# Three edits to an eight-core decoder trunk: norm log and exp as a pair, one weight sum on VectorE, last gates and output projection tile by tile

## The chip, the cores and the metric

The kernel runs on the eight cores of one Trainium2 chip, one launch, no exchange between the cores: each takes one of the eight prompt sequences (2048 tokens) and 16 of the 128 sample sequences (8 tokens each, 128 columns). A core has TensorE (PE: matmuls, PEld its weight loads), VectorE (DVE), ScalarE (ACT), GpSimd (POOL) and SyncE (SP). The metric is the device time in microseconds of the slowest core.

## The reference

```python
def layer(x, c, ...):
    mod = jax.nn.silu(c) @ w_ada + b_ada                 # nine vectors of 1024 for each sequence
    h = rmsnorm(x, n1) * (1 + sc1) + sh1
    x = x + 0.5 * gt1 * swiglu(h, f1g, f1u, f1d)         # 1024 -> 2816 -> 1024
    h = rmsnorm(x, nm) * (1 + sc2) + sh2
    y, ... = token_mixer(h, ...)
    x = x + gt2 * y
    h = rmsnorm(x, n2) * (1 + sc3) + sh3
    x = x + 0.5 * gt3 * swiglu(h, f2g, f2u, f2d)

def token_mixer(h, ...):
    xp, xl, gl, u, v, gates = split(h @ w_in)
    y_pool = pool_mixer(xp, ...); y_lru = rg_lru(causal_conv(xl), ...) * gelu(gl); y_gm = chunk_gmlp(u, v, ...)
    g = sigmoid(gates)                                   # three gates of 1024 channels
    merged = g[0] * (y_pool @ wbo_pool) + g[1] * (y_lru @ wbo_lru) + g[2] * (y_gm @ wbo_gm)
    return merged @ w_out
```

There are four layers and one last RMSNorm. rmsnorm(x) = x * rsqrt(mean(x*x) + 1e-6) * g. New states of pool, convolution and recurrence are outputs too.

## The kernel before

**Tiling.** Activations lie with channels on the partitions: `xT` (f32, the residual stream), `hT` (bf16, the normed input), and three bf16 buffers, seen in the order listings as `R0` (the merged mixer output), `R1`, `R2` (during the last gates the recurrent branch's output); the profile writes all three as `R`. The columns are worked off in two groups. The first is two prompt tiles of 512 columns (called tile 0 and tile 1 here), the second is two more and the sample tile of 128. Each group goes through all four layers: first FFN, mixer, output projection, second FFN. So there are eight passes of each stage.

**A norm.** Each of the eight 128-channel chunks of `xT` is squared on ScalarE; the squares are added on GpSimd, except that the last goes to TensorE beside the sum (`sbt,onesb` matmuls, a mean over channels). Then `rstd` (L818) makes `exp(-0.5*ln(mean+eps))` by two ScalarE activations, which both have the table set lnexp; eight chunks are multiplied by it (two on GpSimd, six on VectorE), and scaled and shifted into `hT` (six on ScalarE, two on VectorE). In an FFN `tsums` (L906) then makes four sums and differences of parts of `hT` on VectorE (L903), since the gate and up products are made by a Strassen-Winograd scheme of seven products of half size.

**Weights** come over GpSimd's DMA queue, converted to bf16, into a ring of 84 pages of 256 columns (`wload`, L671). A gate/up block has 4096 columns and takes 7168, because `wino_load` (L687) adds four sums of 1024: two on VectorE, the third by `W3_ENG`, the fourth by `W4_ENG`, both GpSimd before. An FFN loads 11 such blocks. The first two are used for tile 0, then for the other tiles (`units`, L983 to L986), so that the last tile's norm has matmuls beside it.

**The mixer's end** (L1402 on). For gate branch 1, which reads the recurrent output, channels 0 to 3 are done for all tiles, then 4 to 7 for tile 0, then 4 to 7 for tile 1 (and the sample tile). One `gate_unit` of a prompt tile is eight matmuls on `hT`, eight on `R2`, a tanh on ScalarE, a product on VectorE and an addition into `R0` on GpSimd. Then comes the projection: for each tile eight times eight matmuls on `R0`, each followed by the residual sum into `xT` on VectorE and by the norm's square. Every group of eight needs all eight chunks of `R0` of its tile.

**What sets the order.** All operations are recorded in program order with their dependencies. `schedule` (L247) then runs a list scheduler with cost estimates, and each engine's instructions are written out in the order in which it picked them. Among the ready ones it takes the first by program order for which a PSUM bank or a scratch buffer is free. On ScalarE it passes over an activation whose table set is not loaded, as long as another can run, unless it has been ready for `PATIENCE` (L326). On the chip each engine runs its own list strictly in order, and waits on semaphores.

## Time and profile before

| | |
|---|---|
| three runs | 6855.04, 7126.43, 7339.58 us; median 7126.43 us |
| profiled execution | 6869.45 us, slowest core 7 with a span of 6867.9 us, others from 6830.3 us |
| TensorE | busy 6475.0 us (94%), 46336 matmuls |
| VectorE | busy 3873.2 us (56%) |
| ScalarE | busy 3234.2 us (47%) |
| GpSimd | busy 2576.4 us (38%) |
| granted TensorE clock, core 7 | 0.975 of full speed |
| weights by GpSimd's queue | 539.01 MB, 44.4% of 16 DMA engines |

The page gives for each engine the busy time of the slowest core; a busy TensorE includes matmuls that run at a lower clock. The chain of waits goes back from the last instruction to whatever released each one; 80% of it is matmuls, 7% VectorE, 4% ScalarE, 2% DMA and 6% issue. A timeline row is a run of equal instructions with its start and its duration, and in brackets the idle time of the engine ahead of it and what ended that.

### The profile page before, as it was taken

To read this page: it belongs to the slowest core of one execution; us is meant where nothing else is said; L and a number is where in the kernel's file an instruction comes from. 1 tells how busy PE (TensorE), PEld (TensorE's weight loads), DVE (VectorE), ACT (ScalarE), POOL (GpSimd) and SP (SyncE) were. 2 spreads that over 40 slices of the span, in tenths; PEclk is the share of its full clock that TensorE was granted. 3 is DMA by queue.
4 is the path that set the end of the run, shared out by engine and by line. 5 is a ranking of instruction groups with operands and counts; after the bars stand their busy time and mean duration, and the time that the engine had idled before them with its cause. 6 is when DMAs were issued, how large, how long until landed. Compare 5 with 4: busy or idle time off the path is not lost.

```text
span 6867.9 us, 135354 instructions; the slowest of 8 cores (6830.3 to 6867.9 us)
## 1 busy us (share of the span) xinstructions
PE 6475.0 (94%) x46336; PEld 4093.9 (60%) x46336; DVE 3873.2 (56%) x6064; ACT 3234.2 (47%) x6151; POOL 2576.4 (38%) x2626
## 2 busy tenths in 40 slices
PE   5999999999999999999999999999999999999999
PEld 4644765456744666447754586644767447674466
DVE  4364664655655654755647465464744756556564
ACT  3274444633455433744447444374533744336542
POOL 3245333443334433353433433334322344233442
PEclk9899999999999999999999999999999999999999
DMA  6775546645557356435544342434334443343423
GB/s 123 112 120 100 90 88 119 111 80 108 94 102 127 63 100 119 81 61 97 125 75 93 65 83 54 83 78 77 66 64 77 84 83 58 66 84 73 83 54 81
DMA packets 146674, 600.93 MB, mean 87 GB/s; under 512 B 20944, under 2 KB 53200, under 8 KB 104016
## 3 DMA queue, kind: packets, MB, share of 16 engines
q0 software_dynamic: 89856, 539.01, 44.4%
q1 hardware_dynamic: 56144, 53.27, 3.0%
q8 instruction: 383, 6.28, 0.4%
q14 instruction: 291, 2.38, 0.1%
HBM read 1109.23 MB, written 21.95 MB: 165 GB/s over the span
## 4 chain that ended last, share of the span: by engine, by line
PE 80%; DVE 7%; issue 6%; ACT 4%; DMA 2%; POOL 1%; SPq 1%; DVEq 0%; ACTq 0%; POOLq 0%
PE psum L559 80%; ACT sbt L581 3%; DVE sbt L590 2%; DVE sbt L605 1%; DMA ring<-ffn_gu 1%; DVE sbt L620 1%; ACT L581 1%; DVE xT L605 1%; SPq L627 1%; DVE hT L598 0%; DVE sbt L903 0%; DMA xT<-xp 0%; DVE hT L903 0%; DVE psum L590 0%; POOL sbt L611 0%
## 5 line engine op out<-in xcount | busy, mean ns | idle before, releaser
L559 PE MATMUL psum<-hT,ring 128*128 128x256 bf16 (+2 forms) x21696 | 3207.2, 301 | 175.9 <-ACT sbt L581 32.4
L559 PEld LDWEIGHTS psum<-hT,ring 128*128 128x128 bf16 x21696 | 1994.8, 99 | 1152.8 <-issue 241.0
L581 ACT ACTIVATE sbt<-psum 128x512 f32<-128x512 f32 (+2 forms) x3229 | 1566.0, 509 | 1791.1 <-PE psum L559 1317.1
L559 PE MATMUL psum<-R,ring 128*128 128x512 bf16 (+1 forms) x11520 | 2207.0, 348 | 1.0 <-ACT R L581 0.9
L559 PEld LDWEIGHTS psum<-R,ring 128*128 128x128 bf16 x11520 | 1032.0, 98 | 1083.8 <-issue 28.7
L559 PE MATMUL psum<-sbt,ring 128*128 128x256 bf16 (+2 forms) x9792 | 1307.0, 278 | 107.6 <-ACT sbt L581 50.5
L559 PEld LDWEIGHTS psum<-sbt,ring 128*128 128x128 bf16 x9792 | 934.7, 99 | 322.8 <-issue 158.9
L646 POOL TENSOR_TENSOR ring<-ring 128x1024 bf16<-128x1024 bf16 x352 | 756.6, 2167 | 585.2 <-DVE ring L646 580.2
L605 DVE SCALAR_TENSOR_TENSOR xT<-psum,modT,xT 128x512 f32<-128x512 f32 x384 | 284.0, 748 | 936.1 <-PE psum L559 936.1
L581 ACT ACTIVATE sbt<-xT 128x512 f32<-128x512 f32 (+1 forms) x426 | 266.3, 628 | 1071.6 <-DVE xT L605 992.2
L590 DVE TENSOR_TENSOR psum<-psum,sbt 128x512 f32<-128x512 f32 x704 | 489.8, 697 | 354.8 <-ACT sbt L581 244.6
L590 POOL TENSOR_TENSOR sbt<-sbt 128x512 f32<-128x512 f32 (+1 forms) x316 | 414.9, 1314 | 717.2 <-ACT sbt L581 695.3
L590 DVE TENSOR_TENSOR R<-sbt,psum 128x256 bf16<-128x256 f32 x1144 | 473.4, 416 | 243.8 <-ACT sbt L581 231.4
L605 DVE SCALAR_TENSOR_TENSOR sbt<-sbt,psum 128x512 f32<-128x512 f32 (+1 forms) x288 | 188.4, 656 | 538.9 <-PE psum L559 469.5
L590 POOL TENSOR_TENSOR R<-R,sbt 128x512 bf16<-128x512 bf16 (+1 forms) x288 | 339.1, 1179 | 382.2 <-DVE sbt L605 373.3
L605 DVE SCALAR_TENSOR_TENSOR sbt<-sbt,vecT 128x512 f32<-128x512 f32 (+1 forms) x480 | 348.1, 743 | 134.4 <-ACT convst L581 83.5
L605 DVE SCALAR_TENSOR_TENSOR sbt<-sbt 128x512 f32<-128x512 f32 (+2 forms) x448 | 316.3, 726 | 183.7 <-ACT sbt L581 176.2
L581 ACT ACTIVATE sbt<-sbt 128x256 f32<-128x256 f32 (+1 forms) x577 | 269.9, 482 | 270.5 <-DVE sbt L590 257.8
L581 ACT ACT_TABLE_LOAD x266 | 341.3, 1283 | 116.9 <-PE psum L559 92.5
L590 DVE TENSOR_TENSOR sbt<-xT,sbt 128x512 f32<-128x512 f32 x300 | 323.5, 1128 | 68.4 <-ACT sbt L581 67.7
L627 POOL DMA_DIRECT2D ring<-ffn_gu x176 | 99.7, 567 | 673.2 <-PE psum L559 646.4
L590 DVE TENSOR_TENSOR R<-sbt 128x256 bf16<-128x256 f32 x352 | 212.1, 603 | 152.3 <-ACT sbt L581 150.0
(84 smaller groups left out, 3824.4 us busy)
## 6 DMA issues: line engine op xcount, KB each, us to landing
ring<-ffn_gu POOLq DMA_DIRECT2D x176, 1024.0 KB, 8.9
ring<-ffn_dn POOLq DMA_DIRECT2D x128, 704.0 KB, 8.4
ring<-ada_w POOLq DMA_DIRECT2D x72, 1024.0 KB, 10.7
ring<-w_gate POOLq DMA_DIRECT2D x64, 1024.0 KB, 9.8
ring<-w_lru POOLq DMA_DIRECT2D x64, 576.0 KB, 8.8
ring<-w_gate POOLq DMA_DIRECT2D x32, 768.0 KB, 9.7
ring<-w_pool POOLq DMA_DIRECT2D x32, 640.0 KB, 8.5
ring<-w_o POOLq DMA_DIRECT2D x32, 512.0 KB, 9.6
```

Of the source, the lines that this page charges most:

```text
L559: ins = e.matmul(res(o), lhsT=res(l), rhs=res(r), start=st, stop=sp, skip_group_check=shared)
L581: return S.add("act", lambda e: e.activation(out=res(out), in_=res(in_), func=func, **{k: res(v) for k, v in kw.items()}), reads=rd, write ...
L590: return S.add(eng, lambda e: e.tensor_tensor(out=res(out), in0=res(in0), in1=res(in1), op=op), reads=[in0, in1], writes=[out], cost=dcost ...
L605: return S.add(eng, lambda e: e.scalar_tensor_tensor(out=res(out), in0=res(in0), scalar=scalar, in1=res(in1), op0=op0, op1=op1), reads=rd, ...
L620: return S.add("dve", lambda e: e.tensor_tensor_scan(out=res(out), data0=res(d0), data1=res(d1), initial=res(init), op0=op0, op1=op1), rea ...
L627: return S.add(q, lambda e: e.dma_start(out=res(out), in_=res(in_), **kw), reads=[in_] if reads is None else reads, writes=[out] if writes ...
L646: self.op.append(S.add(eng, lambda e: e.tensor_tensor(out=self.ap, in0=a, in1=b, op=op), reads=[a, b], writes=[self.ap], cost=160.0 + 0.6 ...
```

## The change

Three things are edited. **(1)** In `rstd` both activations are marked urgent: the scheduler may pick them even if their table set is not loaded, and it keeps ScalarE shut for another 25 ns of its own reckoning after the log, so that the exp, ready by then, is the next pick. `PATIENCE` of the others goes from 5000 to 10000. **(2)** The third weight sum of each gate/up block goes to VectorE. **(3)** Gate branch 1 is done for channels 0 to 5 of all tiles; channels 6 and 7 are done tile by tile, each tile's just ahead of its own projection. The load of the last gate block is now recorded behind those of the projection. In the FFN the two hooks, which may each record one step of the conditioning vectors (`ada_slot`), move ahead by one pass of the loop.

```diff
@@ -35,7 +35,7 @@
 HOLD = 4
 ADA0 = {"gu": 0.46, "dn": 1, "mix": 0.5}
 ADA1 = {"dn": 1, "mix": 0.39}
-W3_ENG = "pool"
+W3_ENG = "dve"
 W4_ENG = "pool"
 
 O_XP, O_XL, O_GL, O_U, O_V, O_G0 = 0, 1024, 2048, 3072, 3584, 4096
@@ -131,7 +131,7 @@
 
 class Op:
     __slots__ = ("eng", "fn", "dma", "deps", "signal", "count", "sem", "target", "prev", "cost", "tset",
-                 "prio", "nbytes", "alloc", "pvs", "succ", "nd", "start", "ready", "lat", "idx", "stage")
+                 "prio", "nbytes", "alloc", "pvs", "succ", "nd", "start", "ready", "lat", "idx", "stage", "urgent", "hold")
 
     def __init__(self, eng, fn, dma):
         self.eng, self.fn, self.dma = eng, fn, dma
@@ -141,6 +141,8 @@
         self.sem = None
         self.target = 0
         self.prev = 0
+        self.urgent = False
+        self.hold = 0.0
 
 
 class Sched:
@@ -150,7 +152,7 @@
     PE_LAT = 210.0
     SEM_LAT = 70.0
     TABLE = 1300.0
-    PATIENCE = 5000.0
+    PATIENCE = 10000.0
     RES = {"b": 1, "s": 4}
 
     def __init__(self):
@@ -323,7 +325,7 @@
                         if not can(o):
                             skipped.append(it)
                             continue
-                        if e == "act" and not (o.tset is None or table in o.tset
+                        if e == "act" and not (o.tset is None or table in o.tset or o.urgent
                                                or now - o.ready > self.PATIENCE):
                             if late is None:
                                 late = it
@@ -354,7 +356,7 @@
                         c += self.TABLE
                         table = o.tset[0]
                     o.start = now
-                    free_at[e] = now + c
+                    free_at[e] = now + c + o.hold
                     busy[e] += c
                     self.ops[e].append(o)
                     if o.dma:
@@ -364,7 +366,7 @@
                     else:
                         fin = now + c + (self.PE_LAT if e == "pe" else 0.0)
                     push(fin, 0, o)
-                    push(now + c, 2, o)
+                    push(now + c + o.hold, 2, o)
                 for it in waiting[e]:
                     if it[2].ready == 0.0:
                         it[2].ready = now
@@ -819,8 +821,9 @@
             assert self.k == KC
             r = SB()
             n = self.t.n
-            act(r.f(n), self.pv.c(n), AF.Ln, bias=EPS, scale=1.0)
-            act(r.f(n), r.f(n), AF.Exp, scale=-0.5)
+            ln = act(r.f(n), self.pv.c(n), AF.Ln, bias=EPS, scale=1.0)
+            ln.urgent, ln.hold = True, 25.0
+            act(r.f(n), r.f(n), AF.Exp, scale=-0.5).urgent = True
             return r
 
     def norm_apply(l, which, nm):
@@ -984,8 +987,7 @@
             units(first[jb], jb, grp[:1])
         for jb in range(2):
             units(first[jb], jb, grp[1:])
-        hook("gu")
-        hook("gu")
+            hook("gu")
         for jb in range(2, 11):
             units(wino_load(gu[l, jb], len(grp)), jb, grp)
             hook("gu")
@@ -1399,17 +1401,15 @@
         if last_prompt:
             dma(o_conv_p[l], convst[:, l])
             dma(o_lru_p[l], lrust[:, l])
-        for c, f in gates(1, KC, ylr, range(4)):
+        for c, f in gates(1, KC, ylr, range(6)):
             f()
-        for t in grp:
-            for c, f in gates(1, KC, ylr, range(4, 8), [t]):
-                f()
-
         S.stage = S.stage.replace('mix','wo')
         next_mod(l, 2)
         wos = [wload(w_o[l, q], 2048, 2 * len(grp)) for q in range(4)]
         hook()
         for t in grp:
+            for c, f in gates(1, KC, ylr, range(6, 8), [t]):
+                f()
             nm = Norm(t)
             for m in range(KC):
                 n = t.n
```

The order of the instructions moves with it. **The first place** is the projection of layer 1 in the first group. On TensorE `psum<-hT` x8 with `psum<-R2` x8 is one gate unit, `psum<-R0` the projection (64 for each tile), `sbt,onesb` the norm's mean, the 256-column rows the second FFN. Before:

```order
L559 MATMUL psum<-hT,ring 128x512 x8
L559 MATMUL psum<-R2,ring 128x512 x8
L559 MATMUL psum<-hT,ring 128x512 x8
L559 MATMUL psum<-R2,ring 128x512 x8
L559 MATMUL psum<-hT,ring 128x512 x8
L559 MATMUL psum<-R2,ring 128x512 x8
L559 MATMUL psum<-scT,ring 128x17 x32
L559 MATMUL psum<-R0,ring 128x512 x88
L559 MATMUL psum<-sbt,onesb 128x512 x2
L559 MATMUL psum<-R0,ring 128x512 x40
L559 MATMUL psum<-hT,ring 128x256 x32
L559 MATMUL psum<-sbt,ring 128x256 x16
```

And with the change (line numbers are two higher in the new file):

```order
L561 MATMUL psum<-hT,ring 128x512 x8
L561 MATMUL psum<-R2,ring 128x512 x8
L561 MATMUL psum<-hT,ring 128x512 x8
L561 MATMUL psum<-R2,ring 128x512 x8
L561 MATMUL psum<-R0,ring 128x512 x8
L561 MATMUL psum<-scT,ring 128x17 x32
L561 MATMUL psum<-R0,ring 128x512 x56
L561 MATMUL psum<-hT,ring 128x512 x8
L561 MATMUL psum<-R2,ring 128x512 x8
L561 MATMUL psum<-sbt,onesb 128x512 x2
L561 MATMUL psum<-R0,ring 128x512 x64
L561 MATMUL psum<-hT,ring 128x256 x40
```

The gate units of tile 1 stood all ahead of the first projection. Now one of them stands behind tile 0's 64 matmuls, and right behind it the projection of tile 1, whose input it makes, with only two norm matmuls between. On ScalarE the same place has the log (`sbt<-psum`, one) and the exp (`sbt<-sbt`) of tile 0's norm. Before:

```order
L581 ACTIVATE sbt<-psum 128x512 x22
L581 ACTIVATE sbt<-xT 128x512 x10
L581 ACTIVATE sbt<-psum 128x512
L581 ACTIVATE sbt<-xT 128x512
L581 ACTIVATE sbt<-sbt 128x512
L581 ACTIVATE sbt<-xT 128x512
L581 ACTIVATE hT<-sbt,modT 128x512 x6
```

With the change:

```order
L583 ACTIVATE sbt<-psum 128x512 x22
L583 ACTIVATE sbt<-xT 128x512 x8
L583 ACTIVATE sbt<-psum 128x512 x2
L583 ACTIVATE sbt<-sbt 128x512
L583 ACTIVATE hT<-sbt,modT 128x512 x6
```

A square of tile 1 stood between log and exp, and one more behind the exp ahead of the first scaled chunk (`hT<-sbt,modT`). Neither does now; the log is the second of the two `sbt<-psum`, behind a gate's tanh.

**The second place** is GpSimd's queue there: `R0<-R0,sbt` are the gates' additions, `sbt<-sbt` the norm's sums, `sbt<-xT,sbt` its products, `ring<-ring` weight sums, DMA rows weight loads. Before:

```order
L590 TENSOR_TENSOR R0<-R0,sbt 128x512 x5
L627 DMA ring<-ffn2_gu 128x4096
L590 TENSOR_TENSOR R0<-R0,sbt 128x512 x3
L627 DMA ring<-ffn2_gu 128x4096
L590 TENSOR_TENSOR sbt<-sbt 128x512 x3
L646 TENSOR_TENSOR ring<-ring 128x1024
L590 TENSOR_TENSOR sbt<-sbt 128x512
L646 TENSOR_TENSOR ring<-ring 128x1024
L590 TENSOR_TENSOR sbt<-sbt 128x512 x4
L590 TENSOR_TENSOR sbt<-xT,sbt 128x512 x2
```

With the change:

```order
L592 TENSOR_TENSOR R0<-R0,sbt 128x512 x4
L629 DMA ring<-ffn2_gu 128x4096
L592 TENSOR_TENSOR sbt<-sbt 128x512 x6
L629 DMA ring<-ffn2_gu 128x4096
L592 TENSOR_TENSOR R0<-R0,sbt 128x512
L592 TENSOR_TENSOR sbt<-xT,sbt 128x512 x2
L592 TENSOR_TENSOR sbt<-sbt 128x512 x2
L629 DMA ring<-ffn2_gu 128x4096
L592 TENSOR_TENSOR sbt<-sbt 128x512
L648 TENSOR_TENSOR ring<-ring 128x1024
```

Both loads of the coming FFN stood ahead of the norm's sums of tile 0. Now the second stands behind six of them, and the third ahead of the last sums of tile 1; tile 0's sums are no longer parted by weight sums.

**The third place** is ScalarE at the change from the second FFN to the next layer's first, in the second group (layers 0 and 1). `128x128` rows are the sample tile's log (`sbt<-psum`) and exp (`sbt<-sbt`); 128x256 rows are the FFN's silu or, where read from PSUM, also copies for its products. Before:

```order
L581 ACTIVATE sbt<-psum 128x256
L581 ACTIVATE sbt<-xT 128x512
L581 ACTIVATE sbt<-psum 128x512 x2
L581 ACTIVATE sbt<-psum 128x128
L581 ACTIVATE sbt<-psum 128x256 x2
L581 ACTIVATE sbt<-sbt 128x256
L581 ACTIVATE sbt<-psum 128x512 x2
L581 ACTIVATE sbt<-sbt 128x128
L581 ACTIVATE sbt<-psum 128x512 x2
L581 ACTIVATE sbt<-psum 128x256 x3
```

With the change:

```order
L583 ACTIVATE sbt<-psum 128x256
L583 ACTIVATE sbt<-xT 128x512
L583 ACTIVATE sbt<-psum 128x512
L583 ACTIVATE sbt<-psum 128x128
L583 ACTIVATE sbt<-sbt 128x128
L583 ACTIVATE sbt<-psum 128x512
L583 ACTIVATE sbt<-psum 128x256
L583 ACTIVATE sbt<-psum 128x512 x2
L583 ACTIVATE sbt<-psum 128x256 x2
```

Between log and exp stood five activations of the FFN, among them two runs of 256-column ones; now they follow each other.

## Rows read from the trace of the kernel before

**Rows 1.** Windows over the span, core 7; the first row names the columns.

```profile
core 7: us, PE busy (x) PEld busy (x) DVE busy (x) ACT busy (x) POOL busy (x), PEclk, DMA share, GB/s
...
200.00:6800.00 6600.00, 6307.97 (x44946) 3973.64 (x44944) 3760.71 (x5860) 3148.27 (x5983) 2500.57 (x2543) 0.98 0.47 87
```

**Rows 2.** Window inside the second FFN of layer 1, first group.

```profile
1600.00:1720.00 120.00, 119.35 (x847) 73.17 (x844) 50.30 (x85) 35.83 (x70) 40.03 (x36) 1.00 0.65 113
```

**Rows 3.** Windows at the eight changes from projection to second FFN.

```profile
1478.00:1528.00 50.00, 37.22 (x263) 27.44 (x262) 41.90 (x58) 28.84 (x51) 18.38 (x14) 0.86 0.20 34
...
4822.00:4852.00 30.00, 17.77 (x142) 13.13 (x140) 27.56 (x35) 19.24 (x32) 14.48 (x9) 0.83 0.22 41
...
sum 324.00, PE 222.65 PEld 164.53 DVE 281.32 ACT 190.57 POOL 132.60; mean PE 27.83 PEld 20.57 DVE 35.16 ACT 23.82 POOL 16.58
```

**Rows 4.** Timeline of TensorE at the projection of layer 1, first group.

```profile
1453.02 19.15 PE L559 MATMUL psum<-R,ring 128*128 128x512 bf16 x88
...
1482.46 1.03 PE L559 MATMUL psum<-hT,ring 128*128 128x256 bf16 x8 [1.11 <-ACT hT L581]
1486.42 3.54 PE L559 MATMUL psum<-hT,ring 128*128 128x256 bf16 x16 [2.93 <-DVE xT L605]
...
1505.58 1.03 PE L559 MATMUL psum<-hT,ring 128*128 128x256 bf16 x8 [2.90 <-ACT hT L581]
1508.69 1.87 PE L559 MATMUL psum<-hT,ring 128*128 128x256 bf16 x8 [2.08 <-DVE psum L590]
```

**Rows 5.** Timeline of VectorE, same place: norm products, then residual sums.

```profile
1476.01 4.63 DVE L590 TENSOR_TENSOR sbt<-xT,sbt 128x512 f32<-128x512 f32 x3 [0.70 <-ACT sbt L581]
...
1481.96 1.88 DVE L590 TENSOR_TENSOR sbt<-xT,sbt 128x512 f32<-128x512 f32 x3
...
1484.23 2.71 DVE L605 SCALAR_TENSOR_TENSOR xT<-psum,modT,xT 128x512 f32<-128x512 f32 x4
```

**Rows 6.** Timeline of ScalarE, same place: table load; square between log and exp.

```profile
1472.91 1.28 ACT L581 ACT_TABLE_LOAD   x1 [0.77 <-PE psum L559]
...
1474.69 0.62 ACT L581 ACTIVATE sbt<-xT 128x512 f32<-128x512 f32 x1
```

**Rows 7.** Timeline of GpSimd, same place: weight sum, tile 0's last norm sum.

```profile
1466.47 2.13 POOL L646 TENSOR_TENSOR ring<-ring 128x1024 bf16<-128x1024 bf16 x1
...
1470.49 1.27 POOL L590 TENSOR_TENSOR sbt<-sbt 128x512 bf16<-128x512 f32 x1 [0.20 <-POOL sbt L590]
```

**Rows 8.** Timeline: a gate unit's last matmuls and its addition.

```profile
644.30 1.89 PE L559 MATMUL psum<-R,ring 128*128 128x512 bf16 x8
...
647.20 1.16 POOL L590 TENSOR_TENSOR R<-R,sbt 128x512 bf16<-128x512 bf16 x1 [2.16 <-DVE sbt L605]
```

**Rows 9.** Timeline of ScalarE and TensorE, second group, second FFN to layer 1.

```profile
4200.19 1.28 ACT L581 ACT_TABLE_LOAD   x1
...
4212.90 1.28 ACT L581 ACT_TABLE_LOAD   x1 [0.20 <-PE psum L559]
...
4219.39 1.03 PE L559 MATMUL psum<-sbt,ring 128*128 128x256 bf16 x8 [4.06 <-ACT sbt L581]
```

**Rows 10.** Windows at changes from second FFN to the next layer.

```profile
926.00:941.00 15.00, 8.58 (x48) 5.56 (x47) 13.64 (x19) 7.37 (x13) 5.31 (x3) 0.63 0.01 2
...
4187.00:4222.00 35.00, 24.87 (x239) 20.60 (x237) 28.92 (x41) 21.44 (x34) 9.37 (x7) 0.93 0.30 52
```

**Rows 11.** Groups of instructions by line: weight sums and table loads.

```profile
L646 POOL TENSOR_TENSOR ring<-ring 128x1024 bf16<-128x1024 bf16 x352 | 756.6, 2167 | 585.2 <-DVE ring L646 580.2
...
L646 DVE TENSOR_TENSOR ring<-ring 128x1024 bf16<-128x1024 bf16 x352 | 254.7, 724 | 29.6 <-DMA ring<-ffn_gu 11.8 <-DVE ring L646 10.7 <-PE psum L559 4.0
...
L581 ACT ACT_TABLE_LOAD x266 | 341.3, 1283 | 116.9 <-PE psum L559 92.5
```

**Rows 12.** TensorE's waits for FFN weights, whole span: total, times, longest.

```profile
PE psum L559 <- DMA ring<-ffn_gu: 24.9, 6, 14.3
```

**Rows 13.** The page's part 6: count, KB each, median us to landing.

```profile
ring<-ffn_gu POOLq DMA_DIRECT2D x176, 1024.0 KB, 8.9
```


## The prediction

> **What bounds the kernel now.** I read the windows over the span first. Between 200 and 6800 us TensorE is busy 6307.97 us and idle 292 us, at a mean granted clock of 0.98 [rows 1]. So the whole prize is 292 us of idleness and about 2% of clock; no edit here removes matmuls. Then a window inside an FFN: TensorE 119.35 of 120 us at clock 1.00, VectorE 50.30, GpSimd 40.03 [rows 2]. There nothing but matmuls counts, and a sum moved between the other two engines is free. The idleness lies where the stages change. In the eight windows from the projection to the second FFN TensorE works 222.65 of 324 us, so 101.35 us are idle, 12.7 us at each change, and VectorE is busy 281.32 us, 87% [rows 3]. The clock falls there as well: 0.86 and 0.83 in the two windows shown, against 1.00 in the FFN [rows 2, 3]. That is 50 x 0.14 + 30 x 0.17 = 12.1 us of full-speed work beside 12.78 + 12.23 = 25.0 us of idleness, 0.48 us for each idle us. Since part of a dip belongs to gaps that stay, I let each idle us saved give back 0.4 us more; the factor is 1.4.
>
> Next the timelines at one such change, layer 1 of the first group. The last 88 projection matmuls start at 1453.02 and take 19.15 us, 0.218 us each; 40 more follow [rows 4]. The FFN starts with gaps of 1.11 us (for a scaled chunk of tile 0) and 2.93 us (for the sums behind it), and for tile 1 it waits 2.90 and 2.08 us more [rows 4]. VectorE shows why: tile 0's norm products come in two runs, and four residual sums of tile 1, whose matmuls were done, stand behind them and start at 1484.23 only [rows 5]. Tile 1's norm begins with those.
>
> **Edit 3, gates tile by tile.** The order puts one gate unit of tile 1, 16 matmuls or 16 x 0.218 = 3.48 us, between tile 0's projection and tile 1's. Tile 0's norm has that much more beside it. The change adds a wait, however: tile 1's projection needs the eighth merged chunk, which that unit makes. From the end of its matmuls (644.30 + 1.89 = 646.19) to the end of the addition on GpSimd (647.20 + 1.16 = 648.36) it takes 2.17 us [rows 8]; two norm matmuls cover 0.44, and TensorE, which has all the projection and the FFN queued behind, waits about 1.7 us. Tile 0's norm gains 3.48 + 1.7 = 5.2 us of cover against 1.11 + 2.93 = 4.04 us of gap, so the gap goes: 4.04 - 1.7 = 2.3 us gained. Tile 1's residual sums no longer queue behind the norm: their last ends with its matmuls, at about 1481.2 + 1.7 + 1.0 = 1483.9 instead of 1484.23 + 2.71 = 1486.94 [rows 4, 5], 3.0 us earlier, and nearly all that follows hangs on it. I take 2.5 us for each of the four changes in the first group. In the second group the sample tile's gate unit stands behind tile 1's, so the addition is covered and I take the full 3.5 us, again four times. Sum 24 us of idleness. The nearest bounds are 0 (norm still late) and 4.04 us at each.
>
> The gate's own product and addition are not new work, they move into a crowded stretch: one product on VectorE, one addition of 1.16 us on GpSimd. In return GpSimd's queue loses two weight sums of 2.13 us that stood among tile 0's norm sums, the last of which ended at 1471.76 [rows 7]. I set these against each other.
>
> **Edit 1, log and exp as a pair.** In the order a square stood between them; in the trace it starts at 1474.69, while the log's table load had begun 0.77 us after ScalarE went idle for the norm's matmuls [rows 6]. The square takes 0.62 us, of which about 0.5 us come through, since neighbours overlap a little. Only the last norm of a change hangs on the path: 8 changes into the second FFN, 8 into the mixer, 6 into the next layer, so 22 x 0.5 = 11 us. From a second FFN to the next layer TensorE is idle 15 - 8.58 = 6.4 us in the first group and 35 - 24.87 = 10.1 us in the second, where the sample tile's norm comes last [rows 10]. At the third place of the order, five FFN activations parted the sample tile's log and exp. There the trace has five table loads between 4200.19 and 4214.2, the first and the last of which are shown, and TensorE then waits 4.06 us for ScalarE [rows 9]. With the pair two of the five loads go, 2 x 1.283 us [rows 11]; three such changes at 2.5 us give 7.5 us. `PATIENCE` decides on ties of waiting activations alone; ScalarE has room between changes, so I cost it at nothing, and if that cover is gone at a change it is one load, 1.28 us.
>
> The Trainium skill speaks against this edit (page "ScalarE: Activation LUTs", section "Table sets: the hidden batching unit"): do all activations of one table set before changing to another; a log taken at once breaks into a run of silu. By that rule each norm pays a further pair of loads and the sum comes out near 6900 us instead of 6808; it is a rival below. The page's price of a load, about 1283 ns, the trace bears out [rows 11]; that a log held back saves one, it does not, since the log starts a load as soon as its input is there [rows 6].
>
> **Edit 2, third weight sum.** 176 sums of 2167 ns leave GpSimd, and 176 of 724 ns come to VectorE [rows 11], 127 us in all. Most stand inside an FFN, where VectorE has 70 of 120 us free [rows 2]: nothing. If that cover were gone, all 127 us would count. At the eight changes it is two-sided. VectorE gets two such sums in its crowded stretch (1.4 us); but three norm products take 4.63 us while GpSimd works on its own and 1.88 us when it does not [rows 5], so less work on GpSimd is worth up to 2.75 us. I take the middle, 1.0 us for each, 8 us.
>
> **What gets worse.** Weight loads. The load of the last gate block and the coming FFN's second block move back in GpSimd's queue; the second now stands behind six norm sums of tile 0, where both stood ahead of all of them. It has the rest of tile 0's projection and tile 1's 64 matmuls (14 us) before TensorE wants it, against 8.9 us to land [rows 13] and a few sums of 0.72 and 2.17 us: just enough. TensorE's waits for FFN weights are 24.9 us in six times, longest 14.3 [rows 12]. The trace has no such load at this place; between 0 and 5 us at each change, I take 1.25 us each, 10 us, nearer to nothing because it fits by count. The mixer's other reordering I take at nothing, within 10 us either way: its gaps are small pieces. The hooks shift work, they add none.
>
> **Sum.** Idleness 24 + 11 + 7.5 + 8 = 50.5 us, with the clock 1.4 x 50.5 = 71 us; less 10 us for late weights: 61 us. Against the profiled execution, 6869.45 us with its span of 6867.9, that is **6808 us**, 0.9% less. This execution is near the lowest of the three runs shown (6855.04); their median, 7126.43, lies 3.7% above it. The same ratio on that median would be 7063 us.
>
> **Rivals.**
> - *VectorE takes the place of the wait.* It is busy 87% of those windows, 27.56 of 30 us in one [rows 3]. Then cover on TensorE does not help, and two weight sums and a gate's product there cost 2 us each time: 8 x 2 x 1.4 = 22 us back, 24 x 1.4 = 34 us not gained, 11 not gained for edit 2. 6808 + 67 = 6875 us. Against it: its idle-free run holds norm products slowed by GpSimd. Chance 0.20.
> - *Weights come too late* (the slower side). Place: the start of each second FFN, where the second block is loaded behind tile 0's norm sums. The gains of 71 us are used up when each of eight loads comes 71 / (8 x 1.4) = 6.3 us late. With 10 us each, which the longest wait of 14.3 us [rows 12] allows, it is 112 us lost instead of 10: 6910 us. Against it: few waits for weights now. Chance 0.12.
> - *The batching rule holds.* 22 norms on the path with a pair of loads each, 2 x 1.283 us [rows 11]: 22 x 2.57 x 1.4 = 79 us, and the 15 us of log and exp are not gained: about 6900 us. Chance 0.05.
> - *Both tiles' gaps close.* Once the norms are not held up by each other, all 101.35 us at the eight changes go: 142 us with the clock, instead of 1.4 x 32 = 45. 6808 - 97 = 6711 us. Chance 0.08.
> - *The forecast*: 0.55, with 6770 to 6845 us as its own range.
>
> **Numbers.** The range goes from 6740, half way to all gaps closing, to 7070, which takes in the slower cases on the profiled execution and the forecast on the median of the runs shown. About 2% is what a measurement of this kernel can tell from no change. Below 6732 us lies only the rival with both gaps closed and a corner of the forecast: faster by over 2% 0.10. Over 7007 us needs late weights of 18 us at each change, or work that VectorE never catches up: 0.05. Within 2%: 0.85.
>
> **What would show it.** In the changed profile: (a) the same eight changes idle about 75 us instead of 101, with a clock near 0.88; (b) a gap of 1.5 to 2 us ahead of tile 1's projection in the first group, and none ahead of tile 0's first FFN matmuls; (c) tile 1's residual sums singly, each behind its matmuls, not four in a run; (d) exp right behind log, three table loads instead of five at the third place; (e) VectorE busy 100 to 127 us more in all, GpSimd 380 less, the FFN's inside still over 99% TensorE; (f) waits for FFN weights up by about 10 us. It is wrong if (b)'s second gap stays, if weights take (f) past 60 us, or if gaps open inside the mixer, which I have not costed.

## The result

The profiled execution of the changed kernel took 6779.97 us (slowest core 6, span 6778.4 us; the others from 6761.0 us), against 6869.45 us before. The ratio to the kernel before is **0.9892 [0.985, 0.9935]**, and in a second set of runs (e5 below) 0.9895 [0.9867, 0.9924]: 1.1% faster, between the 0.9% of the forecast (61 us) and the 1.3% between the two profiled executions (89 us). The median of all four runs, 7365.86 us, holds executions in which the cores of one die ran at a granted clock of 0.85 to 0.91; the ratio and the times named below leave them out.

### The profile page after: what moved, and what is told of

Same layout as the page of the kernel before. It is cut to its first block, busy times and chain, and to the rows that moved or that the text cites. A ratio compares the mean times of both kernels' runs of the same rounds, so it can differ in the third digit from the quotient of the medians.

```text
span 6778.4 us, 134693 instructions; the slowest of 8 cores (6761.0 to 6778.4 us)
## 1 busy us (share of the span) xinstructions
PE 6392.8 (94%) x45887; PEld 4069.7 (60%) x46336; DVE 4034.8 (60%) x6240; ACT 3228.0 (48%) x6143; POOL 2203.1 (33%) x2450
## 4 chain that ended last, share of the span: by engine, by line
PE 79%; issue 6%; DVE 6%; ACT 5%; DMA 1%; POOL 1%; SPq 1%; DVEq 0%; ACTq 0%; POOLq 0%
PE psum L561 79%; ACT sbt L583 3%; DVE sbt L592 2%; DVE sbt L607 1%; DVE psum L592 1%; ACT L583 1%; DVE xT L607 1%; DVE sbt L622 1%; DMA ring<-ffn_gu 1%; SPq L629 1%; DVE sbt L906 1%; DVE ring L648 0%; ACT hT L583 0%; DMA xT<-xp 0%; DVE hT L906 0%
## 5 line engine op out<-in xcount | busy, mean ns | idle before, releaser
L561 PE MATMUL psum<-hT,ring 128*128 128x256 bf16 (+2 forms) x21522 | 3148.3, 298 | 140.0 <-ACT sbt L583 29.8
L561 PEld LDWEIGHTS psum<-hT,ring 128*128 128x128 bf16 x21696 | 1974.1, 99 | 1090.4 <-issue 195.9
L561 PE MATMUL psum<-sbt,ring 128*128 128x256 bf16 (+2 forms) x9774 | 1285.9, 276 | 90.0 <-ACT sbt L583 34.1
L648 POOL TENSOR_TENSOR ring<-ring 128x1024 bf16<-128x1024 bf16 x176 | 392.1, 2228 | 584.0 <-DVE ring L648 497.8
L648 DVE TENSOR_TENSOR ring<-ring 128x1024 bf16<-128x1024 bf16 x528 | 491.5, 931 | 39.2 <-DMA ring<-ffn_gu 20.9
L583 ACT ACTIVATE sbt<-sbt 128x256 f32<-128x256 f32 (+2 forms) x577 | 270.5, 482 | 270.7 <-DVE sbt L592 251.4
L592 DVE TENSOR_TENSOR sbt<-xT,sbt 128x512 f32<-128x512 f32 x300 | 309.7, 1083 | 94.9 <-ACT sbt L583 94.9
```

The source lines that it names most:

```text
L561: ins = e.matmul(res(o), lhsT=res(l), rhs=res(r), start=st, stop=sp, skip_group_check=shared)
L583: return S.add("act", lambda e: e.activation(out=res(out), in_=res(in_), func=func, **{k: res(v) for k, v in kw.items()}), reads=rd, write ...
L592: return S.add(eng, lambda e: e.tensor_tensor(out=res(out), in0=res(in0), in1=res(in1), op=op), reads=[in0, in1], writes=[out], cost=dcost ...
L648: self.op.append(S.add(eng, lambda e: e.tensor_tensor(out=self.ap, in0=a, in1=b, op=op), reads=[a, b], writes=[self.ap], cost=160.0 + 0.6 ...
```

## The profile after

From the page of the changed kernel: busy time by engine, and the weight sums (three of a block's four on VectorE now, the fourth on GpSimd).

```profile
PE 6392.8 (94%) x45887; PEld 4069.7 (60%) x46336; DVE 4034.8 (60%) x6240; ACT 3228.0 (48%) x6143; POOL 2203.1 (33%) x2450
...
L648 POOL TENSOR_TENSOR ring<-ring 128x1024 bf16<-128x1024 bf16 x176 | 392.1, 2228 | 584.0 <-DVE ring L648 497.8
L648 DVE TENSOR_TENSOR ring<-ring 128x1024 bf16<-128x1024 bf16 x528 | 491.5, 931 | 39.2 <-DMA ring<-ffn_gu 20.9
```

GpSimd lost 373 us of work. VectorE got 162 us more, not 127: its sums take 931 ns on average where they took 724 [rows 11]. Now the eight windows from projection to second FFN, at the same distances from the FFN's first matmul as in [rows 3] (columns as there); layer 1 of each group is shown.

```profile
1433.00:1483.00 50.00, 40.14 (x303) 30.91 (x302) 44.46 (x63) 27.98 (x52) 20.74 (x14) 0.90 0.14 25
...
4756.00:4786.00 30.00, 25.86 (x238) 21.72 (x236) 28.14 (x46) 19.42 (x38) 5.19 (x4) 0.94 0.23 44
...
sum 324.00, PE 268.84 PEld 217.09 DVE 283.13 ACT 193.54 POOL 96.98; mean PE 33.60 PEld 27.14 DVE 35.39 ACT 24.19 POOL 12.12
```

TensorE is idle 324 - 268.84 = 55.2 us there, not 101.35. But part of that has moved ahead of the windows. TensorE's timeline at layer 1, first group (answers to [rows 4]), and then one row of the second group:

```profile
1420.65 0.59 PE L561 MATMUL psum<-sbt,onesb 128*128 128x512 bf16 x2
1423.36 13.97 PE L561 MATMUL psum<-R,ring 128*128 128x512 bf16 x63 [2.12 <-POOL R L592]
1437.17 2.96 PE L561 MATMUL psum<-hT,ring 128*128 128x256 bf16 x24
1445.56 3.39 PE L561 MATMUL psum<-hT,ring 128*128 128x256 bf16 x16 [5.43 <-ACT sbt L583]
...
4754.57 0.63 PE L561 MATMUL psum<-sbt,onesb 128*128 128x512 bf16 x1 [3.89 <-DVE sbt L906]
```

The wait for the eighth merged chunk is there (2.12 us), tile 0's first FFN matmuls start at once, and 24 matmuls later TensorE stops for 5.43 us. In the second group 3.89 us now lie ahead of the FFN. All four layers of each group have such a wait: 1.99 to 2.12 us in the first, 3.89 to 3.92 us in the second. VectorE (answers to [rows 5]) and GpSimd, same place:

```profile
1424.22 4.07 DVE L592 TENSOR_TENSOR sbt<-xT,sbt 128x512 f32<-128x512 f32 x3 [2.54 <-ACT sbt L583]
...
1428.66 1.88 DVE L592 TENSOR_TENSOR sbt<-xT,sbt 128x512 f32<-128x512 f32 x3
...
1430.92 3.37 DVE L607 SCALAR_TENSOR_TENSOR xT<-psum,modT,xT 128x512 f32<-128x512 f32 x5
...
1437.28 4.55 DVE L648 TENSOR_TENSOR ring<-ring 128x1024 bf16<-128x1024 bf16 x1
1441.75 1.74 DVE L906 TENSOR_TENSOR sbt<-hT 128x1024 bf16<-128x1024 bf16 x1
1443.42 0.74 DVE L607 SCALAR_TENSOR_TENSOR xT<-psum,modT,xT 128x512 f32<-128x512 f32 x1
```

```profile
1436.70 1.28 POOL L592 TENSOR_TENSOR sbt<-sbt 128x512 f32<-128x512 f32 x1
1437.94 2.11 POOL L648 TENSOR_TENSOR ring<-ring 128x1024 bf16<-128x1024 bf16 x1
1440.02 1.25 POOL L592 TENSOR_TENSOR sbt<-sbt 128x512 f32<-128x512 f32 x1
```

One weight sum, 0.685 us when alone, takes 4.55 us on VectorE: it ends half a microsecond after a run of three GpSimd instructions. The FFN's first sum of parts of `hT` and tile 1's last residual sum stand behind it. ScalarE's square of that chunk waits 5.34 us for the residual sum, and the copy from PSUM that TensorE needs stands behind the square. That is TensorE's 5.43 us, which the profile puts down to ScalarE:

```profile
1444.30 0.63 ACT L583 ACTIVATE sbt<-xT 128x512 bf16<-128x512 f32 x1 [5.34 <-DVE xT L607]
```

ScalarE (answers to [rows 6]) has log and exp as a pair, and TensorE's waits (total, times, longest) show the new one and fewer for weights than in [rows 12]:

```profile
1421.43 1.28 ACT L583 ACT_TABLE_LOAD   x1 [1.55 <-PE psum L561]
1422.73 0.60 ACT L583 ACTIVATE sbt<-psum 128x512 f32<-128x512 f32 x1
1423.41 0.63 ACT L583 ACTIVATE sbt<-sbt 128x512 f32<-128x512 f32 x1
```

```profile
PE psum L561 <- DVE psum L592: 29.7, 65, 2.2
...
PE psum L561 <- DMA ring<-ffn_gu: 17.4, 5, 14.9
PE psum L561 <- POOL R L592: 10.1, 8, 2.1
```

The first of these rows is new in kind: before, TensorE waited for VectorE's emptying of a PSUM bank 7 times, now 65 times. Nearly all lie inside the FFNs, most of them 0.3 us long. Here is one, on three engines (GpSimd, VectorE, TensorE):

```profile
1542.80 2.13 POOL L648 TENSOR_TENSOR ring<-ring 128x1024 bf16<-128x1024 bf16 x1
1543.31 2.18 DVE L648 TENSOR_TENSOR ring<-ring 128x1024 bf16<-128x1024 bf16 x1
...
1546.35 1.03 PE L561 MATMUL psum<-hT,ring 128*128 128x256 bf16 x8 [0.32 <-DVE psum L592]
```

VectorE's third weight sum starts beside GpSimd's fourth and takes 2.18 us instead of 0.69; the sum from PSUM that stands behind it comes late, and TensorE waits 0.32 us for the bank. A product of the FFN can be caught as well (VectorE, GpSimd, TensorE):

```profile
1509.83 2.09 DVE L592 TENSOR_TENSOR R<-sbt 128x256 bf16<-128x256 f32 x1
1511.84 0.41 DVE L592 TENSOR_TENSOR R<-sbt,psum 128x256 bf16<-128x256 f32 x1
```

```profile
1509.52 2.11 POOL L648 TENSOR_TENSOR ring<-ring 128x1024 bf16<-128x1024 bf16 x1 [4.00 <-DVE ring L648]
```

```profile
1513.74 1.03 PE L561 MATMUL psum<-sbt,ring 128*128 128x256 bf16 x8 [0.60 <-ACT sbt L583]
```

The product `R<-sbt`, both of whose inputs lie in SBUF, takes 0.42 us alone and 2.09 us here; it ends 0.3 us after GpSimd's sum. The one behind it, with an input in PSUM, takes its usual 0.41 us. TensorE waits 0.60 us, for a copy of ScalarE, which itself had sat idle 0.85 us for VectorE's next sum in PSUM.

## The experiments

Two theories ran through them. **A** is the forecast's: each edit is worth its own term, and GpSimd's work slows VectorE's. **B** names the rival for each run. For comparison I cut every core's execution into stages by TensorE's order and take the median of the eight cores: time in the first FFN's gate/up part, in mixer with projection, and in the second FFN's gate/up part, summed over all passes. Beside it stand *holes*: by how much successive weight loads of TensorE lie more than 300 ns apart, over a usual 218 ns. "Starts" are the FFNs before their fourth weight block, "inside" is from it on. The entries depend on where a stage is cut: other cuts move single ones, and some differences between kernels, by up to 20 us, so they say where time went and not how much to the microsecond.

| kernel | profiled, us | ratio | 1st FFN | mixer + proj. | 2nd FFN | holes: starts | inside | mixer + proj. |
|---|---|---|---|---|---|---|---|---|
| before | 6869.45 | 1 | 1316 | 2812 | 1314 | 195 | 21 | 182 |
| changed | 6779.97 | 0.9892 | 1297 | 2809 | 1257 | 138 | 45 | 164 |
| e1 gates alone | 6810.15 | 0.9924 | 1323 | 2820 | 1256 | 164 | 23 | 174 |
| e2 pair alone | 6838.64 | 0.9966 | 1317 | 2800 | 1305 | 192 | 27 | 168 |
| e9 pair, old PATIENCE | 6845.24 | 0.9977 | 1312 | 2802 | 1312 | 194 | 26 | 166 |
| e3 one sum alone | 6849.33 | 0.998 | 1299 | 2815 | 1314 | 176 | 44 | 183 |
| e4 changed, sum back | 6795.15 | | 1317 | 2815 | 1245 | 159 | 28 | 165 |
| e10 changed, both sums | 6720.98 | | 1267 | 2820 | 1214 | 109 | 11 | 169 |
| e14 both sums alone | 6800.86 | | 1280 | 2817 | 1277 | 152 | 12 | 179 |
| e16 changed, sums swapped | 6776.71 | 0.9885 | 1292 | 2814 | 1255 | 140 | 41 | 167 |
| e7 changed, products moved | 6782.20 | 0.9887 | 1278 | 2797 | 1291 | 139 | 42 | 178 |
| e13 = e10 and e7 | 6710.75 | 0.9781 | 1250 | 2800 | 1246 | 107 | 12 | 185 |

**The three edits one by one.** e1 is the kernel before with the edit of the gates only:

```diff
-        for c, f in gates(1, KC, ylr, range(4)):
+        for c, f in gates(1, KC, ylr, range(6)):
...
         for t in grp:
+            for c, f in gates(1, KC, ylr, range(6, 8), [t]):
+                f()
             nm = Norm(t)
```

> The kernel before with edit 3 alone (gate branch 1 channels 6 and 7 tile by tile). Theory A (cover): the eight changes from projection to second FFN lose 2.5 to 3.5 us of idleness each, with the clock 34 us in all, less some 10 us for later weight loads: ratio to before 0.996 (0.993 to 0.999). A wait of about 2 us for GpSimd's addition stands ahead of tile 1's projection in each of the four layers of the first group. Rival B (the hold of GpSimd on VectorE is what costs): cover does little, ratio 1.000. Rival C (any new order of the scheduler is worth 10 to 20 us either way): the difference lies in the mixer, not in the second FFN.

Measured: 0.9924 [0.9905, 0.9944], 52 us, more than either theory gave. e2 is the kernel before with edit 1, PATIENCE included, as the change's diff has it; e3 has edit 2 alone:

```diff
-W3_ENG = "pool"
+W3_ENG = "dve"
```

> The kernel before with edit 1 alone (log and exp as an urgent pair, patience 10000). Theory A: half a microsecond at each of 22 changes and two table loads less at three, 18.5 us of idleness, 26 us with the clock: ratio 0.996. Rival (the batching of table sets holds): slower by up to 79 us, ratio 1.005 to 1.011, with more than 266 table loads. Rival B: ratio 0.999 to 1.000, since norms wait for VectorE and GpSimd and not for ScalarE.

> The kernel before with edit 2 alone (third weight sum on VectorE). Theory A: 8 to 11 us faster, ratio 0.998 to 0.999. Rival B (a VectorE instruction with both inputs in SBUF is held up while GpSimd works; the changed kernel shows a weight sum of 4.55 us instead of 0.68): the relief of norm products and the sums that are caught set each other off, ratio 0.998 to 1.003, and the mean of VectorE's weight sums rises from 724 ns to over 850.

Measured: 0.9966 [0.9949, 0.9984] and 0.998 [0.9967, 0.9992]. Of 6869 us the three ratios make 52 + 23 + 14 = 89 us (1.3%); all together give 1.1%, with an interval of 0.4% on either side. So the runs show no interplay of the edits, and could not show one below some 0.4%. The move of the two hooks is in none of the three; it came with every kernel that starts from the changed one, and was not run by itself. e4 takes edit 2 out of the changed kernel again (the same line the other way round).

> The changed kernel with the third weight sum back on GpSimd. Its profiled span was 6778 us against 6868 before, ratio of fast runs 0.989. Theory A: 10 us more than the changed kernel, ratio to before 0.991. Rival B: the weight sum of 4.55 us that holds up tile 1's last residual sum in the first group goes, 10 to 20 us less than the changed kernel: ratio 0.986 to 0.988. If the three edits add up, e1, e2 and e3 give the 1.1% together; if not, this run and the next tell which pair belongs together.

It took 6795.15 us, 15 us more than the changed kernel where A has 10, but the table shows B's picture behind the small sum: edit 2 gains 20 us of holes at the starts (159 to 138) and loses 17 inside (28 to 45). e3 shows the same alone: 195 to 176, and 21 to 44. e5 is the changed kernel once more, as the measure for the next runs; its ratio stands at the top, its holes are 136 and 45.

> The changed kernel itself, unchanged, beside the next three on one chip. Ratio to before 0.989 (0.987 to 0.991), profiled spans within 10 us of 6761 to 6778.

**Where VectorE is held up.** e6 lets GpSimd make the third sum again for the first two blocks of each second FFN, e7 gives all norm products to VectorE, e8 does both.

```diff
-        first = [wino_load(gu[l, jb], len(grp)) for jb in range(2)]
+        first = [wino_load(gu[l, jb], len(grp), "pool" if which else W3_ENG) for jb in range(2)]
```

```diff
-N_POOL = (3, 6)
+N_POOL = ()
```

> The changed kernel, but the first two gate/up blocks of each second FFN make their third sum on GpSimd again; all other blocks keep it on VectorE. With all of them back (e4) the second FFNs took 12.6 us less (1244.8 against 1257.4 us by the cores' medians) and the first FFNs 19.8 us more. Theory B (a VectorE sum that is caught by GpSimd holds up tile 1's residual sums, and only at this change): both gains are kept, 10 to 15 us less than the changed kernel, ratio to before 0.987, and no weight sum of over 3 us on VectorE at the eight changes. Rival (the difference is the scheduler's new order): 0 within 5 us, ratio 0.989.

> The changed kernel with all eight norm products of a prompt tile on VectorE, none on GpSimd. Theory B (GpSimd's work beside VectorE's two-input sums is what stretches them): eight products of 0.63 us and two scalings of 0.54 make 6.1 us from the exp to the last chunk, against 4.07 + 0.54 + 1.88 + 0.54 = 7.0 us for six now; 1 to 2 us less at each of 22 changes, 30 us with the clock, ratio to before 0.985. Theory A (VectorE is the crowded engine, at 87% of those windows): two more products there cost 1.3 us at each change, 40 us with the clock, ratio 0.995.

e6's lowest time was 6811.76 us, six of its cores with spans of 6765.8 to 6784.6 us, against 6785.84 us and 6761.7 to 6784.3 us in e5. So no gain, as its rival has it. e7: 0.9887 [0.9858, 0.9915], no different. The products fell from 1083 to 737 ns and the first FFNs won 19 us, but in the second group the order that came with it cost 23 us between the mixer's start and the second FFN's end.

> e6 and e7 together. If both gain by separate means the ratio to before is 0.983; if e7's gain is the same stretch that e6 cures, it equals the better of the two.

Four cores of e8's profiled execution, at a granted clock of 0.989 to 0.991, had spans of 6747.5 to 6761.0 us. e11 is the same kernel:

> The kernel of e8 once more (the changed kernel with all norm products on VectorE, and the third weight sum of the first two blocks of each second FFN on GpSimd), whose undisturbed cores had spans of 6747.5 to 6761.0 us. Theory A (both moves take VectorE's slow sums out of GpSimd's way or the reverse at different places, so they add up): slowest undisturbed core 6755 to 6765 us, ratio 0.985 to 0.988 against the kernel before, and the lowest time below the changed kernel's 6779.97. Rival B (only the products count, as in e7): 6775 to 6782 us, ratio 0.9885.

6762.22 and 6772.0 us, as A has it: below e7's 6780.1 and 6782.2, although e6 by itself gained nothing. Why the two together gain is open.

**The pair and PATIENCE.** e9 is e2 with PATIENCE left at 5000.

> The kernel before with edit 1 but PATIENCE left at 5000. With both, the pair gave a ratio of 0.9966, 23 us off the execution of before; of that the median cores had about 12 us in the first group's four mixers (1200.0 to 1188.0) and 8 in the second group's second FFN or nothing, so the gain may not be the norm's. Theory A (the log and the exp as neighbours shorten the norms, as predicted, 22 norms on the path): the gain stays, ratio 0.996 to 0.998, the slowest core's span 6835 to 6850 us, and the first group's mixers stay near 1190. Rival B (the mixer's order under the longer PATIENCE gave it): the first group's mixers go back to 1200 us, the table loads on the median core go up by 8 or more from 254, and the ratio is 0.998 to 1.001.

0.9977 [0.9964, 0.999]: the pair itself gains, 16 us, and the rest may be PATIENCE's, though the intervals of e2 and e9 overlap. The table has the place: the starts' holes are unchanged (195, 194), the mixer's fall from 182 to 166. The table loads are 254 in e9 as in e2, so it is the pair that saves them.

**The new wait.** e12 makes the addition of gate branch 1, channels 6 and 7, on VectorE (32 additions for prompt tiles and 4 for sample tiles in the whole run; the count in the expectation is wrong).

```diff
-            tt(mg, mg, go, ALU.add, eng="pool")
+            tt(mg, mg, go, ALU.add, eng="dve" if br == 1 and m >= 6 else "pool")
```

> The changed kernel with the gates' addition into the merged output on VectorE for branch 1, channels 6 and 7 (20 additions for prompt tiles and 4 for sample tiles in four layers: 16 + 16 + 4 in all), so that tile 1's projection no longer waits for GpSimd's. Theory A (the new wait of 2.1 us ahead of tile 1's projection in each of the first group's four layers is the hop over GpSimd, and it is on the path): the wait shrinks to 0.5 to 1.2 us, four times, worth 4 x 1.2 x 1.4 = 7 us less what VectorE's added work costs there; ratio against the kernel before 0.987 to 0.989. Rival B (the wait only hides VectorE's queue, which tile 0's norm fills): the wait shrinks, but the gaps inside the second FFN's start grow by the same, or the addition stands in VectorE's queue behind residual sums and the wait stays at 2 us; time that of the changed kernel within 5 us.

```profile
1425.27 13.97 PE L561 MATMUL psum<-R,ring 128*128 128x512 bf16 x64 [1.38 <-DVE R L592]
```

The wait shrank to 1.38 us and the kernel got slower: 0.9912 [0.9883, 0.994], 6799.63 us at best against 6779.97. The second FFNs took 1276 us instead of 1257, so rival B, and more: work given to VectorE at this place, with the order that came with it, costs more than the wait it removes.

**A second dose of edit 2.** e10 is the changed kernel with the fourth sum on VectorE as well:

```diff
-W4_ENG = "pool"
+W4_ENG = "dve"
```

> The changed kernel with the fourth weight sum on VectorE as well: a second dose of edit 2, 176 more sums of about 0.93 us as the changed kernel's rows have them, 164 us more on VectorE, 390 us less on GpSimd. Theory A (GpSimd's work slows VectorE's sums of two SBUF tiles, and inside an FFN VectorE has room): the ring sums' mean falls below 0.85 us, since less GpSimd work runs beside them, the first FFNs take no longer than 617 + 680 us in the two groups, and the time is that of the changed kernel or up to 12 us less. Rival B (VectorE is full at the changes, and in the first FFNs of the second group too): each of the eight second FFNs gets two more sums of 0.7 to 0.9 us in its first blocks, 8 x 1.6 x 1.4 = 18 us longer, most of it in the second FFNs (601 + 656 us), ratio near 0.992.

6720.98 us, 59 us less than the changed kernel: neither theory had half of it. From its page:

```profile
PE 6407.5 (95%) x46336; PEld 4074.8 (61%) x46336; DVE 3968.8 (59%) x6416; ACT 3235.3 (48%) x6143; POOL 1807.5 (27%) x2274
...
L648 DVE TENSOR_TENSOR ring<-ring 128x1024 bf16<-128x1024 bf16 x704 | 496.1, 715 | 35.1 <-DMA ring<-ffn_gu 24.3
```

VectorE makes 176 more sums and is busy 66 us **less**: 704 sums of 715 ns take about as long as the changed kernel's 528 of 931, and everything else that GpSimd's sums held up is faster too. Windows of 70 us that start 60 us after the second FFN's first matmul, layer 1, first group, in the kernels before, changed and e10:

```profile
1542.43:1612.43 70.00, 69.40 (x636) 61.76 (x634) 49.43 (x93) 33.81 (x78) 28.70 (x18) 1.00 0.48 92
```

```profile
1496.96:1566.96 70.00, 68.39 (x622) 60.17 (x620) 56.91 (x99) 34.98 (x79) 16.64 (x12) 1.00 0.45 84
```

```profile
1486.62:1556.62 70.00, 69.94 (x638) 62.03 (x637) 54.45 (x104) 34.79 (x79) 3.70 (x7) 1.00 0.53 95
```

(The first row is the kernel before, the second the changed one, the third e10.) TensorE is idle 0.60, 1.61 and 0.06 us. VectorE has 21, 13 and 16 us free; it is not full, it is held at the wrong moment. Before, GpSimd's two sums cost about 0.5 us in this window as well, which I had read as nothing: in e14, the kernel before with both sums on VectorE, TensorE is idle 0.08 us there. Earlier weight loads, which GpSimd issues, are not what e10 gains: TensorE's waits for them are 19.7 us, 17.4 in the changed kernel.

Four more runs settled the cause. e14 is the kernel before with both sums on VectorE and nothing else, e15 is e10 again, e16 the changed kernel with third and fourth sum swapped between the engines, e13 is e10 with e7's `N_POOL = ()`.

> The kernel before with both weight sums on VectorE and nothing else. Theory A (the collision of the two sums is the whole difference between e3 and this): e3 was 0.998; the collision's 20 us inside the FFNs go and the starts gain as in e10 against the changed kernel, so that the time is 45 to 60 us below e3's, 6790 to 6805 us, ratio 0.990 to 0.993, and VectorE's ring sums average 0.70 to 0.75 us. Rival B (VectorE only has the room because the gates' order gives it): 6835 to 6850 us, as e3, with the starts of the second FFNs longer than in e3.

> The kernel of e10 once more. Theory A (the gain is real): lowest time 6715 to 6730 us and, if enough undisturbed runs come, a ratio of 0.978 to 0.982 against the kernel before. Rival B (the one run of e10 was a lucky one): 6750 us or more.

> The changed kernel with the third weight sum on GpSimd and the fourth on VectorE: the same number of sums on each engine, the other one on each. Theory A (both sums are released by the second and start together, so one on each engine collide whichever it is): VectorE's ring sums average 0.88 to 0.95 us as in the changed kernel (0.931), the FFNs' insides keep their holes, and the time is within 8 us of the changed kernel's (6779.97 to 6788.34). Rival B (the third sum on VectorE is the trouble, since it is made first and holds VectorE's queue): average below 0.80, and the time 6740 to 6765 us.

> The kernel of e10 (both weight sums on VectorE) with the norm's products all on VectorE as well, as in e7. Theory A (what slows VectorE at the changes is GpSimd's work of any kind beside its sums and products of two SBUF tiles): the gain of e7 in the first FFNs (19 us in the first groups' stage times) comes on top of e10, lowest time 6700 to 6715 us, and no ring sum on VectorE takes over 1.5 us. Rival B (e7 took the second group's seconds back by its other order, and e10 has already removed the collisions): time 6715 to 6735, no better than e10's 6720.98.

The times of all four came out as theory A. e14: 6800.86 us, 48 below e3, holes inside 12. e15: 0.9796 [0.9769, 0.9823]. e16: 0.9885 [0.9848, 0.9922], sums of 969 ns, holes inside 41: it does not matter which of the two is on GpSimd (A had 880 to 950 ns). TensorE's waits for a PSUM bank number 62 in e16, 53 in e3, 14 in e14, 7 in e10:

```profile
PE psum L561 <- DVE psum L592: 8.6, 7, 2.2
```

e13 is the best kernel of the study, **0.9781 [0.9745, 0.9818]**, 6707.93 us. Its products:

```profile
L592 DVE TENSOR_TENSOR sbt<-xT,sbt 128x512 f32<-128x512 f32 x392 | 264.8, 727 | 125.2 <-ACT sbt L583 125.2
```

392 of them take less than 300 did in the changed kernel (309.7 us). One part of its expectation failed: the slowest of its weight sums still took 2.21 us. GpSimd keeps the sums of squares and the gates' additions.

## Why the forecast held, and which steps did not

The total on the profiled execution was right (0.9% forecast, 1.1% measured), but by luck: its terms were wrong in both directions, and the errors set each other off. The main step that failed is in edit 2, "most stand inside an FFN, where VectorE has 70 of 120 us free: nothing". The runs showed 17 to 23 us of TensorE's idleness there, made by GpSimd's sum holding up VectorE's.

- **The ratio carried to the median, 7063 us, inside a range up to 7070: measured 7365.86.** The step that failed is that the median of the runs would move with the kernel. With the fourth run of the kernel before that came with the result (6856.6 us) its median is 6991.52 us; the changed kernel's is 5% above it while the kernel got faster. What moves it stands under the result and is no effect of the edits.
- **Edit 3, 24 us of idleness, 34 with the clock: measured 52 (e1).** At the changes it did less than forecast. Holes of the second FFNs' starts and the projection together: in the second group from 52 to 39, 13 us for my 14; in the first from 66 to 62, not 10. The step of the first group that failed is "tile 1's residual sums no longer queue behind the norm". Tile 0's norm keeps VectorE until 1430.9 in the changed kernel, 7.5 us into tile 1's projection, and five residual sums stand behind it. The rest came from the mixer, which I had put "at nothing, within 10 us either way": its holes, without the projection's, fell by 27 us (167 to 140), two thirds of them in the second group. There the recurrence's units had 42 us of holes before and 23 in e1. The gates' move reordered the mixer; which of its moves did it I have not isolated. The table's column hides this, since the projection's holes rose from 15 to 34; in stage times mixer with projection took 8 us more and the second FFNs 58 us less.
- **(b) the wait of 1.7 us ahead of tile 1's projection: right**, 1.99 to 2.12 us, four times. That tile 0's first matmuls have no gap ahead: right. That the gap then is gone: wrong, it stands 24 matmuls later (5.43 us) for the weight sum of edit 2, and layers 0 and 2 have two gaps there (1.6 and 2.3, 2.1 and 3.0 us). "It is wrong if (b)'s second gap stays", the prediction said, and so it was. (a) 55 us in the windows instead of about 75, but the new waits lie ahead of them, 3.9 us at each change of the second group and 2.1 of the first: 55.2 + 4 x 3.9 + 4 x 2.1 = 79 us. The clock, 0.90 and 0.94 in the two windows shown, rose as forecast (0.88) and more. (c) wrong: five residual sums in a run.
- **Edit 1, 18.5 us of idleness, 26 with the clock: measured 23 (e2), 16 without PATIENCE (e9).** The size was right, the place wrong: next to nothing in the holes at the starts of the FFNs (195 to 192), the rest in the mixer, though by stage time e2's second FFNs took 9 us less (e9's 2). (d) right: at the third place three table loads stand instead of five (4137.69, 4140.55, 4143.03), and 258 in all. The rival that the batching rule of the Trainium skill holds fell: with both activations taken at once the kernel has fewer table loads (254 in e2, 266 before [rows 11]) and is faster. The rule (page "ScalarE: Activation LUTs", section "Table sets: the hidden batching unit") is to batch activations by table set; here the log had broken into the run of silu before the change too, and only the exp was late. (The rival's own sum was off: it took 15 us for log and exp where the terms are 18.5, 26 with the clock, so its time is about 6913 us.)
- **Edit 2, 8 us at the changes and nothing inside, 11 with the clock: measured 14 (e3).** The starts gained about 20 us of holes, not 8, and the insides lost 17 to 23, not 0. The failed step is "inside an FFN VectorE has 70 of 120 us free: nothing". Free time does not help an instruction that is held while TensorE waits for its bank. At the changes the relief was underrated in turn, since I priced it by the norm products alone. (Nor was 1.0 us "the middle": with two sums of 0.7 us against up to 2.75 us of relief the bounds were -1.4 and +1.35.) The Trainium skill had the mechanism (page "SBUF — State Buffer", section "SBUF: two separate sides"): GpSimd and a VectorE instruction with two SBUF inputs take turns at one port pair, each for its whole length. The trace agrees: 0.42 us becomes 2.09 beside a GpSimd sum of 2.11, and an instruction with an operand in PSUM is spared. I had the slow products in [rows 5] and left it at a middle value.
- **Late weights, 10 us lost: nothing.** 17.4 us of waits, 24.9 before (f). The loads had the room that I had counted.
- **(e)** GpSimd 373 us less (380 forecast), VectorE 162 more (100 to 127): its weight sums alone took 237 us more (254.7 to 491.5), the rest of its work 75 less. That the FFN's inside stays over 99% TensorE was wrong: 68.39 of 70 us is 97.7%.
- Rival "VectorE binds" gave the right engine at the changes (e12 suggests that added work there costs) and the wrong reason. Its cure is not less work on VectorE but less on GpSimd.

## What to carry to other kernels

When work is moved between GpSimd and VectorE, look at what each does *while* the other works, not at their busy shares: in these traces VectorE instructions with both inputs in SBUF stop while GpSimd's sums run, and a sum moved over alone (e3, 20 us between the profiled executions) is worth far less than both moved together (e14, 69 us). A mean that rises when a group grows (724 to 931 ns for the same shape) is the sign to look for. And a total that comes out right proves no term: edit the parts one by one, and compare holes stage by stage.

## What the runs showed of the hardware

- A VectorE instruction can wait through several GpSimd instructions, not one: 4.55 us beside 1.28 + 2.11 + 1.25 us issued back to back. It did not get in between them.
- Of the forms of VectorE's work compared here, only those without a PSUM operand suffer. In the changed kernel the sums `psum<-psum,sbt` average 695 ns and in e10, with 396 us less work on GpSimd, 697; products with a PSUM input 415 and 415 ns. Sums of two SBUF tiles go from 931 to 715, `R<-sbt` from 543 to 425.
- The granted clock over the whole execution was 0.986 on the changed kernel's slowest core and 0.987 on e10's. So e10's 59 us are idleness, and its holes are 58 us fewer in the three columns of the table; the forecast's factor of 1.4 for the clock does not apply there. Between the kernel before (0.975) and the changed one the clock did rise, and 51 us fewer holes came with 89 us less time between the slowest cores, 78 us between the medians of the cores.
